# Hybrid decoder layer: near HGRN scores packed in one PSUM bank and spread by transfers, outer decays computed anew, root by logarithm

## What is computed

```python
def hgrn2_chunked(q, k, v, log_f):
    ...
    bc = jnp.cumsum(gc, axis=-2)
    ...
        diff = bi[..., :, None, :] - bi[..., None, :, :]
        decay = jnp.exp(jnp.where(causal, diff, -jnp.inf))
        scores = jnp.einsum("bhtd,bhsd,bhtsd->bhts", qi, ki, decay)
        o = (jnp.einsum("bhts,bhsv->bhtv", scores, vi)
             + jnp.einsum("bhtd,bhdv->bhtv", qi * jnp.exp(bi), state))
...
    u = lax.linalg.triangular_solve(system, vc * betac[..., None], left_side=True,
                                    lower=True, unit_diagonal=True)
```

## Time and profile before

| | |
|---|---|
| median of 3 runs | 1417.77 us (1417.52 to 1419.52) |
| profiled execution | 1420.56 us, of which 1418.8 us are the profile's span |
| TensorE busy over the span | 1401.1 us, 99% |
| VectorE | 1031.2 us, 73% |
| ScalarE | 704.5 us, 50% |
| GpSimd | 226.1 us, 16% |
| the scan | about 418 to 558 us of the span |
| in it, 418 to 557 us | TensorE 131.5, VectorE 127.1, ScalarE 118.7, GpSimd 118.0 us busy |

### The profile page before, as it was taken

The page is one execution under the profiler, slowest core; times in us unless marked ns, Lnnn a source line. Parts: engine busy times, 40 slices in busy tenths (PEclk is TensorE's granted clock), DMA queues, the critical chain, the costliest instruction groups (busy, mean ns, idle before and its releaser), DMA issues.

```text
span 1418.8 us, 20665 instructions
## 1 busy us (share of the span) xinstructions
PE 1401.1 (99%) x7683; PEld 1171.1 (83%) x7683; DVE 1031.2 (73%) x1522; ACT 704.5 (50%) x1309; POOL 226.1 (16%) x239
## 2 busy tenths in 40 slices
PE   9999999999999999999999999999999999999998
PEld 8877888888878998888888888888888888888886
DVE  7594545562148997368988999999999686577567
ACT  6343456422258896258653344343435444454455
POOL 4000001101038885010000000000000254400000
PEclk9999999999999999999999999999999999999999
DMA  7431323544623332645342344334327765424223
GB/s 241 105 74 30 45 80 116 154 112 108 166 72 108 121 120 83 216 149 184 105 126 82 119 136 139 111 104 160 108 89 259 240 195 196 135 82 134 90 61 148
DMA packets 153251, 181.06 MB, mean 128 GB/s; under 512 B 21241, under 2 KB 92095, under 8 KB 153152
## 3 DMA queue, kind: packets, MB, share of 16 engines
q1 hardware_dynamic: 153152, 179.74, 40.8%
HBM read 130.43 MB, written 49.28 MB: 127 GB/s over the span
## 4 chain that ended last, share of the span: by engine, by line
PE 93%; DVE 3%; ACT 1%; issue 1%; DMA 1%; POOL 0%; SPq 0%; DVEq 0%; ACTq 0%; POOLq 0%
PE psum L2468 9%; PE psum L2470 9%; PE psum L2469 9%; PE psum L2407 5%; PE psum L2408 5%; PE psum L2409 5%; PE psum L674 4%; PE psum L676 4%; PE psum L675 4%; PE psum L2380 4%; PE psum L2381 4%; PE psum L2382 4%; PE psum L1373 3%; PE psum L734 3%; PE psum L732 3%; PE psum L733 3%
## 5 line engine op out<-in xcount | busy, mean ns | idle before, releaser
L166 DVE TENSOR_TENSOR w_wlo<-w_raw,w_whi 128x1024 fp32r<-128x1024 f32 x66 | 86.8, 1317 | 228.1 <-ACT w_whi L151 228.0
L151 ACT ACTIVATE w_whi<-w_raw 128x1024 fp32r<-128x1024 f32 x66 | 69.7, 1058 | 175.4 <-PE psum L2382 79.0
L3201 DVE TENSOR_TENSOR g_slot<-w_raw,g_slot 128x512 fp32r<-128x512 f32 x77 | 69.5, 902 | 51.6 <-ACT g_slot L2775 51.5
L2775 ACT ACTIVATE g_slot<-w_raw 128x512 fp32r<-128x512 f32 x77 | 48.7, 632 | 104.8 <-PE psum L2409 99.6
L674 PE MATMUL psum<-h_hi,w_whi 128*128 128x512 f32 x256 | 100.6, 393 | 0.0
L676 PE MATMUL psum<-h_hi,w_wlo 128*128 128x512 f32 x256 | 99.7, 390 | 0.0
L675 PE MATMUL psum<-h_lo,w_whi 128*128 128x512 f32 x256 | 99.7, 389 | 0.0
L3459 POOL TENSOR_TENSOR mixed_home<-mixed_home 128x512 f32<-128x512 f32 x11 | 16.0, 1455 | 507.0 <-DMA mixed_home<-in_w_down 505.0
L2380 PE MATMUL psum<-w_whi,m_hi 128*128 128x512 f32 x224 | 87.8, 392 | 0.0
L2382 PE MATMUL psum<-w_whi,m_lo 128*128 128x512 f32 x224 | 87.2, 389 | 0.0
L2381 PE MATMUL psum<-w_wlo,m_hi 128*128 128x512 f32 x224 | 87.2, 389 | 0.0
(11 more groups left out here) (446 smaller groups left out, 3967.0 us busy)
## 6 DMA issues: line engine op xcount, KB each, us to landing
w_raw<-in_w_up SPq DMA_DIRECT2D x39, 512.0 KB, 4.0
w_raw<-in_w_in SPq DMA_DIRECT2D x36, 512.0 KB, 6.2
s_rows<-pair_work SPq DMA_DIRECT2D x11, 1024.0 KB, 4.1
w_raw<-s_rows SPq DMA_DIRECT2D x44, 256.0 KB, 2.7
g_rows<-pair_work SPq DMA_DIRECT2D x18, 512.0 KB, 2.6
w_raw<-g_rows SPq DMA_DIRECT2D x33, 256.0 KB, 4.2
w_raw<-in_w_out SPq DMA_DIRECT2D x16, 512.0 KB, 4.1
mixed_home<-in_w_down SPq DMA_DIRECT2D x32, 256.0 KB, 4.4
```

## The change

1. Scores 0 to 5 ("near") are made in blocks of 32 keys by 32 or 16 queries, all into one PSUM bank, each score with a part of its own. VectorE waits for score 5 and copies them in six masked steps, each waiting for the one before, into a packed tile `s_h_near` (two of them, used in turn). Score 6 is copied beside them. Score 7 goes straight to `s_h_scores`. Both are plain copies.
2. SyncE spreads the packed tile over `s_h_scores` by four transfers within SBUF, one for each 32 partitions (`sp_unpack`). "oh" waits for all four.
3. Level 0: for neighbouring positions the decay is the query's own f = 1 - k. ScalarE computes it from k; VectorE's difference and GpSimd's multiplication of keys are gone. Level 6: ScalarE takes the exponentials from the cumulated sums with the middle as bias, in eight activations of 64 columns; VectorE's difference is gone.
4. The root is exp(-0.5 ln(x)) from one table set, which is loaded once ahead of the chunks; the reciprocal on VectorE is gone.
5. `y32` and `dt32` are made as two halves of 64 by 64, `dx`, `y64` and `dt64` with 64 rows where 128 or less were used. The copy after `dx` is a plain one of 32 partitions.
6. Score 0 of the next chunk moves from behind score 2 to behind "hd". GpSimd still multiplies the decayed queries.

Core of the diff:

```diff
-    SCORE_BANK = (0, 7, 3, 6, 1, 7, 2, 7)
+    NEAR_BANK, SCORE_BANK = 0, {6: 1, 7: 7}
+    NEAR, MIDDLE = LEVELS - 2, P // 2 - 1
...
+    def sp_unpack(self, sp, c):
+        self.banks.released(sp, ("score", c, LEVELS - 1))
+        self.banks.released(sp, ("near", c))
+        if c:
+            self.done(sp, ("oh", c - 1))
+        sc, near = heads(self.sc[:]), self.near_heads(c)
+        for b in range(P // SB):
+            rows, width = slice(b * SB, (b + 1) * SB), SB if b % 2 else 2 * SB
+            sp.dma_start(sc[rows, :, b * SB:b * SB + width], near[rows, :, 0:width]).then_inc(self.s["unpacked"], 16)
...
                 self.load_part(sp, "at", c + 1, self.at)
+            self.sp_unpack(sp, c)
+            if c + 1 < NT:
                 self.done(sp, ("hd", c))
                 self.load_rows(sp, "v", c + 1, 2 * DG, self.hv)
...
-        self.pe_products(pe, ("dt32", c), self.bank("dt32", c), lambda h: self.hs(self.y, h), lambda h: self.hs(xt, h),
-                         (SB, 1), self.DT_ROWS[0])
+        self.pe_halves(pe, ("dt32", c), self.bank("dt32", c), lambda h: self.hs(self.y, h), lambda h: self.hs(xt, h), 1)
...
+    def pe_halves(self, pe, key, bank, left, right, side):
+        out = self.banks.open(pe, key, bank)
+        for h in range(NH):
+            for half in range(2):
+                rows = slice(half * 2 * SB, (half + 1) * 2 * SB)
+                cols = slice(rows.start + side * SB, rows.start + (side + 1) * SB)
+                ins = pe.matmul(self.hs(out, h)[rows, cols], left(h)[rows, rows], right(h)[rows, cols], start=True, stop=True)
...
-            for h in range(NH):
-                for b in range(P // size if n < LEVELS else 1):
-                    keys = slice(b * size, (b + 1) * size - (1 << (n - 1)))
-                    queries = slice(b * size // 2, (b + 1) * size // 2)
-                    ins = pe.matmul(self.packed(out)[keys, h, queries], hs(self.kl[at], h)[:, keys],
-                                    self.packed(self.ql[at])[:, h, queries], start=True, stop=True)
...
+        if n <= self.NEAR:
+            out = self.near_part(self.banks.of(("near", c)), n)
             for h in range(NH):
-                for b in range(P // size):
-                    part = slice(b * size, (b + 1) * size)
-                    ins = pe.matmul(hs(out, h)[part, part], kk[:, h, part], q[:, h, part], start=True, stop=True)
-            self.multiplied.mark(ins, ("score", c, n))
+                for b in range(P // SB):
+                    keys, queries = slice(b * SB, (b + 1) * SB), slice(b * SB // 2, (b + 1) * SB // 2)
+                    left = hs(self.kl[at], h)[:, keys] if n > 1 else kk[:, h, keys]
+                    right = self.packed(self.ql[at])[:, h, queries] if n else q[:, h, keys]
+                    ins = pe.matmul(out[keys, h, :], left, right, start=True, stop=True)
+        else:
+            out = self.packed(self.banks.open(pe, ("score", c, n), self.SCORE_BANK[n]))
+            for h in range(NH):
+                for b in range(P // (2 * ahead)):
+                    keys = slice(2 * b * ahead, (2 * b + 1) * ahead)
+                    ins = pe.matmul(out[keys, h, 0:ahead], hs(self.kl[at], h)[:, keys],
+                                    self.packed(self.ql[at])[:, h, b * ahead:(b + 1) * ahead], start=True, stop=True)
...
-        for n in range(1, LEVELS + 1):
-            self.banks.released(pe, ("score", c, n))
+        pe.wait_ge(s["unpacked"], (c + 1) * (P // SB) * 16)
+        self.banks.released(pe, ("score", c, LEVELS))
...
-            self.pe_score(pe, c + 1, 0)
...
             self.pe_hgrn(pe, c)
+            self.pe_score(pe, c + 1, 0)
             self.pe_score(pe, c + 1, 1)
...
-        m = 1 << lv
-        act.wait_ge(self.s["differed"], c * LEVELS + lv + 1)
-        for side, sign in ((0, -1.0), (1, 1.0)):
-            here = self.front.level_view(self.ed[(c * LEVELS + lv) % 3][:], m, side)
-            ins = act.activation(here, here, ACT.Exp, scale=sign)
...
+        if lv == 0:
+            act.wait_ge(self.front.s["bounded"], 2 * NH)
+            ins = act.activation(self.blocks(heads(ed[:]), m, 1), self.blocks(self.part(self.front.kk, c), m, 1), ACT.Copy,
+                                 scale=-1.0, bias=1.0)
+        elif lv == LEVELS - 1:
+            b = self.part(self.front.f, c)
+            act.wait_ge(self.s["middles"], 1)
+            for h in range(NH):
+                at = c * NH + h
+                act.activation(self.hs(ed, h)[:, 0:m], b[:, h, 0:m], ACT.Exp, scale=-1.0, bias=b[:, h, m - 1:m])
+                ins = act.activation(self.hs(ed, h)[:, m:P], b[:, h, m:P], ACT.Exp, bias=self.middle[:, at:at + 1])
+        else:
+            act.wait_ge(self.s["differed"], c * self.NEAR + lv)
+            act.activation(side(ed[:], 0), side(ed[:], 0), ACT.Exp, scale=-1.0)
+            ins = act.activation(side(ed[:], 1), side(ed[:], 1), ACT.Exp)
...
-        act.activation(self.column(1), self.column(0), ACT.Sqrt, bias=self.k.eps[:, 0:1],
+            act.wait_ge(self.s["inverted"], c)
+        act.activation(self.column(1), self.column(0), ACT.Ln, bias=self.k.eps[:, 0:1],
                        scale=1.0 / HD).then_inc(self.s["rooted"], 1)
+        act.wait_ge(self.s["rooted"], 2 * c + 1)
+        act.activation(self.column(2), self.column(1), ACT.Exp, scale=-0.5).then_inc(self.s["rooted"], 1)
...
+    def dve_near(self, dve, c):
+        self.done(dve, ("score", c, self.NEAR))
+        if c >= 2:
+            dve.wait_ge(self.s["unpacked"], (c - 1) * (P // SB) * 16)
+        bank, blocks = self.banks.of(("near", c)), self.near_heads(c)[:, :, 0:SB]
+        for n in range(self.NEAR + 1):
+            if n:
+                dve.wait_ge(self.s["placed"], c * self.NEAR + n)
+            mask, m = self.k.near[:, n, :].bitcast(U32), 1 << max(n - 1, 0)
+            mask = mask.unsqueeze(1).broadcast_to([P, NH, SB])
+            data = self.near_part(bank, n)
+            if n:
+                side = lambda ap: self.blocks(ap, m, 1)
+                ins = dve.copy_predicated(side(blocks), side(mask), data.rearrange("p h (n m) -> p h n m", m=m))
+            else:
+                ins = dve.copy_predicated(blocks, mask, data)
+            if n == self.NEAR:
+                self.banks.release(ins, ("near", c))
+            else:
+                ins.then_inc(self.s["placed"], 1)
...
+        data = self.packed(self.banks.of(key))[0:P - ahead, :, 0:ahead]
+        if n == LEVELS:
+            if c:
+                self.done(dve, ("oh", c - 1))
+            ins = dve.tensor_copy(heads(self.sc[:])[0:ahead, :, ahead:P], data)
         else:
-            ins = dve.copy_predicated(heads(self.sc[:]), over_heads(k.ident[:].bitcast(U32)), heads(self.banks.of(key)))
+            ins = dve.tensor_copy(self.near_heads(c)[0:P - ahead, :, SB:2 * SB], data)
...
-        if 0 in sides:
+        if 0 in sides and lv:
```

132 lines of the change are left out of this document (67 added, 65 removed).

## The result

The changed kernel takes **1443.88 us** in the median (1442.63 to 1445.82, 4 runs), the kernel before 1418.64 us beside it (1417.52 to 1420.21): the ratio is 1.0178, with an interval of 1.0161 to 1.0196. It is slower by 25 us where 4 us less was predicted, and outside the range.

A forecast was written before the change was run, and what follows sets the result against it. TensorE was taken to bound the kernel, with VectorE, ScalarE and GpSimd close. Six full chunks -1.1, chunk 7 -2.4, chunk 0 +0.1, first inverse -0.8: -4.2 us off 1417.77, so 1413.6 us; forecast 1411 to 1416, range 1407 to 1427.

The forecast's parts named there:

- Near scores, 0.35 us on four tiles: TensorE, scores 0 to 5: four column tiles run side by side, 0.35 us a score in place of 0.49.
- y32, dt32 and dx, 0.6, 0.6 and 0.55: TensorE, inverse in halves: these times in us, saving 0.5 on y32 and 0.4 on the pair dt32 and dx.
- The first inverse: Ahead of the scan, in dense work that TensorE bounds: 0.8 us less.
- Copies of the near scores 1.4 us, level 6 in 1.9: VectorE's six masked copies take 1.4 us; ScalarE's eight activations of level 6 take 0.24 each, 1.9.
- The wait of 0.45 for "vn": TensorE ahead of "gd": ready at 8.7 us into the chunk, but held until 9.15 by ScalarE's copy behind level 6.
- The path to the queue: Chunk from its first state product: solve at 5.7 us, "gd" 9.15, og ended 12.0, SyncE issues "at" 0.1 later.
- Landing 1.8 us: SyncE's transfers within SBUF: 1.8 us from issue to landing, taken from between 1.3 and 2.8.
- rival 1: Transfers land late, 2.3 to 2.5 us, each of seven chunks loses 0.5 to 0.7: a wash, 1418 us; chance 0.22.
- an issue holds the queue for 0.32 us ... I count 0.36: SyncE's queue: 0.36 us an issue with its gap, so the fourth transfer goes out 1.44 us after "at".
- rival 2: TensorE's clock falls to half at the new standing time ahead of "oh": 1430 us, or 1424; chance 0.16.
- VectorE "isn't late any more, so this is worth what it moves": VectorE in the scan: some 3 us of a chunk go, worth only what they move on the path.
- Rivals 3 and 4: Near scores: four tiles not side by side, 1422 or 1431 us, chance 0.08; VectorE's six copies over 3 us, small.

The follow-up runs named there:

- e2_filled: Changed kernel with ten products, whose result is overwritten, on TensorE ahead of the waits of "oh": 1428.58 us, 1.0068 to the kernel before.
- e8_root_alone: Kernel before with only the root by logarithm and exponential: 1418.26 us, 1.0001.
- e9_halves_root: Kernel before with the inverse in halves and the root by logarithm: 1417.59 us, 0.9989.
- e10_all_but_near: Kernel before with all of the change but the packed near scores and their transfers, and "vn" ahead of level 6: 1413.05 us, 0.9962.
- e1_unpack_first: Changed kernel with the four transfers ahead of the load of "at" in SyncE's queue: 1422.65 us, 1.0033 to the kernel before.
- e12_states_first: Changed kernel: transfers ahead of "at", score 6's copy and "vn" earlier, all state products and "hd" ahead of the wait: 1409.82 us, 0.9943 to the kernel before.
- e5_spread_dve: Changed kernel with four copies on VectorE in place of the four transfers: 1435.19 us, 1.0127 to the kernel before.
- e13_one_transfer: Changed kernel with one 128-partition transfer to a tile aside in place of four, near scores not placed: 1427.41 us, 1.0054 to the kernel before.
- e11_late_scores: Changed kernel with "hd" and the first state product ahead of TensorE's wait for the transfers: 1425.27 us, 1.0047 to the kernel before.
- e6_spread_dve_vn_first: Changed kernel with VectorE copies in place of the four transfers, and "vn" ahead of level 6: 1439.71 us, 1.0156 to the kernel before.

## Why the prediction was wrong, point by point

- *Near scores, 0.35 us on four tiles.* 0.38. Right: 32 passes within it, 12 ns each, so the four tiles do run side by side. By the floor of 25 ns in the Trainium skill (TensorE: Matmul & The Clock Gate, "Wait — 56ns, not 53.3ns?") it would have been 0.8, an estimate from that page; the trace does not agree for passes on different tiles.
- *y32, dt32 and dx, 0.6, 0.6 and 0.55.* 0.59, 0.49 and 0.63. Right. The first inverse, from y32 to the solve, fell from 33.75 (386.56 to 420.31) to 33.16 us: 0.6, 0.8 was taken.
- *Copies of the near scores 1.4 us, level 6 in 1.9.* 0.30 + 1.43 and eight at 0.24. Right. The wait of 0.45 for "vn" measured 0.39 in three chunks and less or nothing in the others.
- *The path to the queue.* From "hd" at 478.70 the solve starts 6.04 later (5.7 was taken), "gd" 9.22 (9.15), score 7 12.06 (12.0), and "at" is issued at 12.17 (12.1). Everything up to the transfers was right within 0.1 us, but for the solve, 0.3 late (a gap of 0.17 stands ahead of it).
- *Landing 1.8 us.* For the fourth transfer, which "oh" waits for, 1.8 in six chunks. Right there, so rival 1 was not it; but 2.5 in chunk 4 and 3.1 in chunk 7, which costs 2.0 us.
- **The step that failed: "an issue holds the queue for 0.32 us ... I count 0.36".** It was taken from loads of DRAM to 128 partitions; within SBUF it is 0.60, 0.64 with the gap. The fourth issue starts 2.44 us behind "at" (472.39 to 474.83), not 1.44. That is the first microsecond of the wrong wait; longer issues (up to 1.7 us) add to it in some chunks. TensorE stands 21.5 us in eight chunks; the prediction had 1.1 in six and 0.8 in the last; with 1.1 for chunk 0 too it is 8.5. Of the 13.0 us between, 9.5 are the later start of the fourth issue, summed over the chunks, 2.0 are the late landings above, and 1.5 were not followed. Landing had got a range from 1.3 to 2.8; the issue had got a single number, though the trace of before holds loads of 0.43 directly behind another.
- **And behind it, rival 2, priced well and held too unlikely.** With waits of 2.2 to 3.6 us the clock falls in most chunks; that is 12.9 us by the traces, and 15.3 by `e2_filled`, which saves some long issues as well. The rival's condition (1.7 us and above) was named for a late landing, and its 16% came from landing alone.
- *The rest.* The miss is 1443.9 - 1413.6 = 30.3. Standing and clock are 13.0 + 12.9 = 25.9 of it (the 15.3 would count the long issues twice). The table load that moves to the tail costs 1.2 (`e8_root_alone`): the prediction had said that nothing outside the scan is touched. The first inverse's 0.2 makes 27.3, and 3.0 us stay open. The profiled execution has a gap of 1.70 us in the front, ahead of a product at 382.91, which no other kernel here shows at this place; whether it belongs to the changed kernel or to that execution is not known.
- *VectorE "isn't late any more, so this is worth what it moves".* It holds for the changed kernel (81.0 of 122 us busy), but it leaves out that VectorE was a bound before. A full chunk takes 17.2 us with the halves (`e9_halves_root`), as without them, and 16.74 once the differences of levels 0 and 6 go as well (`e10_all_but_near`, which also moves "vn").
- *Rivals 3 and 4.* Excluded by the rows of the near scores (0.38) and their copies (0.30 + 1.43).

## What to carry to other kernels

An added transfer has three prices, and each wants its own range: the time it holds its queue, the landing, and what the engine that waits for it does meanwhile. Take the hold from an issue with the same kind of source and target and with the same neighbour in the queue; the 0.32 us of a load that stands alone said little here for a transfer within SBUF behind another. And price a new wait on TensorE twice where it is longer than about one microsecond, for the clock behind it. Before moving transfers about, look which of its own products need not wait. Here that alone turned 1444 into 1425 us, and with the order of the queues into 1410.

## What the runs showed of the hardware

- SyncE's issue of a transfer from SBUF to SBUF holds its queue for 0.60 us with 32 partitions and 0.47 with 128 (single ones up to 1.7). A load of 128 partitions from DRAM holds it for 0.32 alone, 0.43 directly behind another load (`before`, 474.56) and 0.59 directly behind a transfer within SBUF (`e1_unpack_first`, 484.76). Why is open.
- Within SBUF, 16 to 32 KB land 1.8 to 3.1 us after issue in the changed kernel, 2.0 in the median, and up to 3.9 in `e12_states_first`. 128 KB land after 2.8 to 4.7 us, 2.9 in the median.
- A copy from SBUF to SBUF on VectorE takes 0.22 to 0.28 us alone and 0.66 to 1.21 beside GpSimd's products, whose instruction it outlasts. A copy from PSUM was not held: 0.28 us beside one of 1.72 (`e5_spread_dve`, 487.05).
- TensorE's granted clock fell to 0.50 at standing times from 1.01 us (`e10_all_but_near`, chunk 7, at 543.3) and 1.24 (`e13_one_transfer`, chunk 1) up to 3.64, but not at 1.53 (`e11_late_scores`, chunk 3), 2.24 (changed kernel, chunk 2) nor 2.54 (`e6_spread_dve_vn_first`, chunk 0). So the length of the last standing time alone does not tell.
- State products of four heads may be started in one PSUM bank, the first with the start flag alone, and the score products added to them later: `e12_states_first` computes so.
